# Identity products in five TensorE waits of a two-layer transformer step, and a later start for part of its constants

## What is computed

```python
sh1, sc1, g1, sh2, sc2, g2 = split(silu(cond) @ w_ada[l] + b_ada[l], 6)   # one cond for context, one for latents
h = rms_norm(x, norm1_g) * (1 + sc1) + sh1
q_lat, ckv_raw, krope, conv_in, na_qkv = split(h @ w_in)
q = rms_norm(rms_norm(q_lat, q_a_g) @ w_q_up); k, v = from(rms_norm(ckv_raw) @ w_kv_up, krope)
o = concat(attention(q, k, v), conv_module(conv_in), neighbourhood_attention(na_qkv))
x = x + g1 * (o @ w_out)
h = rms_norm(x, norm2_g) * (1 + sc2) + sh2
x = x + g2 * moe(h)        # sigmoid router, 16 experts in 4 groups, two of one group per token
```

## Time and profile before

| | |
|---|---|
| median of 3 runs | 1256.28 us |
| the profiled execution's own time | 1256.0 us |
| its span in the profile | 1254.2 us |
| TensorE (PE) busy | 1127.8 us, 90% of the span |
| VectorE (DVE) busy | 885.6 us, 71% |
| ScalarE (ACT) busy | 657.8 us, 52% |
| GpSimd (POOL) busy | 260.3 us, 21% |
| chain that ended last | PE 66%, DVE 21%, DMA 6%, issue 4% |
| mean granted TensorE clock | 0.931 of full speed |

### The profile page before, as it was taken

The page is one execution under the profiler, slowest core; times in us unless marked ns, Lnnn a source line. Parts: engine busy times, 40 slices in busy tenths (PEclk is TensorE's granted clock), DMA queues, the critical chain, the costliest instruction groups (busy, mean ns, idle before and its releaser), DMA issues.

```text
span 1254.2 us, 15896 instructions
## 1 busy us (share of the span) xinstructions
PE 1127.8 (90%) x6102; PEld 918.6 (73%) x6102; DVE 885.6 (71%) x1115; ACT 657.8 (52%) x910; POOL 260.3 (21%) x218
## 2 busy tenths in 40 slices
PE   5999998989689999999969898788949999999985
PEld 2787767678568888888857775577847888888863
DVE  1138177642579999998963767871378999998894
ACT  2222154431268788888833124442237778888870
POOL 5001110210114122212153021101021322212133
PEclk9999998979889999999989997787969999999997
DMA  9965774732489999999943321014358999999951
GB/s 359 305 230 206 300 318 182 276 153 100 168 298 373 353 385 383 370 388 386 396 175 86 120 77 63 4 41 168 117 208 332 357 377 380 375 379 376 372 245 51
DMA packets 54174, 320.72 MB, mean 256 GB/s; under 512 B 11498, under 2 KB 11610, under 8 KB 18896
## 3 DMA queue, kind: packets, MB, share of 16 engines
q1 hardware_dynamic: 38448, 276.59, 57.6%
q0 software_dynamic: 15648, 43.08, 9.4%
HBM read 313.40 MB, written 25.44 MB: 270 GB/s over the span
## 4 chain that ended last, share of the span: by engine, by line
PE 66%; DVE 21%; DMA 6%; issue 4%; ACT 1%; POOL 1%; SPq 0%; DVEq 0%; POOLq 0%; ACTq 0%
PE bank L1121 33%; PE bank L821 10%; PE bank L1034 6%; DVE w_lo L2109 5%; PE bank L810 4%; DMA ring<-wring_dram 3%; DVE conv_acc L1905 3%; PE bank L927 2%; PE bank L1113 2%; PE bank L899 2%; DMA late<-y_rows 2%; PE bank L832 1%; PE bank L913 1%; DVE rowmax L1705 1%; PE bank L865 1%
## 5 line engine op out<-in xcount | busy, mean ns | idle before, releaser
L2109 DVE TENSOR_TENSOR w_lo<-ring,w_hi 128x2048 fp32r<-128x2048 f32 x190 | 433.5, 2300 | 44.2 <-ACT w_hi L1420 44.0
L1420 ACT CAST w_hi<-ring 128x2048 fp32r<-128x2048 f32 x192 | 367.0, 1917 | 34.1 <-PE bank L1121 33.7
L1121 PE MATMUL bank<-w_hi,hgT_hi 128*128 128x512 f32 x512 | 204.5, 399 | 5.3 <-issue 3.4
L1121 PE MATMUL bank<-w_hi,hgT_lo 128*128 128x512 f32 x512 | 201.3, 393 | 0.0
L1121 PE MATMUL bank<-w_lo,hgT_hi 128*128 128x512 f32 x512 | 200.8, 392 | 0.0
L821 PE MATMUL bank<-ring,hT 128*128 128x256 f32 (+1 forms) x672 | 140.7, 370 | 0.4 <-issue 0.4
L821 PEld LDWEIGHTS bank<-ring,hT 128*128 128x128 f32 x672 | 122.6, 191 | 16.5 <-issue 1.9
L1121 PE MATMUL bank<-w_hi,hidT_hi 128*128 128x512 f32 x256 | 103.9, 406 | 18.9 <-DVE y_split L2163 18.9
L720 POOL DMA_INDIRECT y_rows<-y,y_at x26 | 47.1, 1810 | 353.2 <-ACT y L1451 353.2
L1121 PEld LDWEIGHTS bank<-w_hi,hgT_hi 128*128 128x128 f32 x512 | 97.0, 190 | 26.5 <-issue 7.2
L1121 PEld LDWEIGHTS bank<-w_hi,hgT_lo 128*128 128x128 f32 x512 | 96.9, 189 | 21.0
(11 more groups left out here) (266 smaller groups left out, 1596.3 us busy)
## 6 DMA issues: line engine op xcount, KB each, us to landing
ring<-wring_dram SPq DMA_DIRECT2D x260, 1024.0 KB, 8.4
y_rows<-hg POOLq DMA_DIRECT2D x6, 1024.0 KB, 7.2
kT<-mod_dram POOLq DMA_DIRECT2D x4, 1024.0 KB, 8.5
late<-y_rows POOLq DMA_DIRECT2D x4, 1024.0 KB, 14.4
ring<-wring_dram SPq DMA_DIRECT2D x6, 640.0 KB, 7.6
h_rows<-h_tok POOLq DMA_DIRECT2D x6, 512.0 KB, 3.0
bias<-na_bias_dram POOLq DMA_DIRECT2D x32, 64.0 KB, 4.9
A<-mod_dram POOLq DMA_DIRECT2D x2, 1024.0 KB, 5.0
```

Source lines behind the costliest of these rows:

```text
L1121: mm = pe.matmul(b[:, :], a, w[m], start=(start and k == 0), stop=(stop and k == 2))
L1420: act.copy(w_hi[:, q, :], in_ring(l, expert_slot(e, i))).then_inc(hi_made[q], 1)
L2109: dve.tensor_tensor(w_lo[:, q, :], in_ring(l, expert_slot(e, i)), w_hi[:, q, :], ALU.subtract) \
```

## The change

A new helper on TensorE, `keep_busy(l, key, count)`, waits until the bank that `key` names is free and then multiplies the identity by the identity `count` times into its first 128 columns. It raises no semaphore, nobody reads the result, and the next real product into that bank starts a new accumulation. It stands in five places of each layer, ahead of the waits listed above: 3 products (layer 0) or 14 (layer 1) behind the latents' transposes, 9 behind the mix transposes, 26 behind the last score product, 7 before each of the first two lists, 8 before the first expert's tokens.

At the start, layer 0's order on TensorE is rewritten: `turn_mod` of a pair comes between the two slots of the next pair, and the transposes of tiles 0 and 1 come before the eighth slot's products. `psum_plan` follows. Of the constants only the shapes and `vecs` are issued at first; triangle, row ids, router weights and bias, rotary tables, mask and the two tables are issued by GpSimd after `mod_ready`, ahead of the small transfers and the bias, which thereby also come after `mod_ready`. VectorE waits for the later constants behind the modulation of tile 2 and makes there what depends on them.

```diff
+IDLE_ROUTER, IDLE_LISTS, IDLE_GATHER, IDLE_MIX, IDLE_LATENTS = 26, 7, 8, 9, (3, 14)
...
+        for i, (m, k) in enumerate(FIRST_PAIRS):
+            order += [("ada", m, 2 * k)]
+            if i:
+                order += [("mod", *FIRST_PAIRS[i - 1])]
+            if i == len(FIRST_PAIRS) - 1:
+                order += first_turns
+            order += [("ada", m, 2 * k + 1)]
+        order += [("mod", *FIRST_PAIRS[-1])]
...
-        N_CONST = 16 * 8
+        N_CONST, N_CONST_LATER = 16 * 2, 16 * 6
...
-            pool.dma_start(triangle, shape_consts[:, 2, :]).then_inc(consts_loaded, 16)
-            pool.dma_start(wr[:], w_router).then_inc(consts_loaded, 16)
-            pool.dma_start(br[:], b_router.partition_broadcast(P)).then_inc(consts_loaded, 16)
-            pool.dma_start(ropes[:], rope).then_inc(consts_loaded, 16)
-            pool.dma_start(mask[:], na_mask).then_inc(consts_loaded, 16)
-            pool.dma_start(ids[:], row_ids).then_inc(consts_loaded, 16)
...
-            for n in range(DEPTH):
-                pool.dma_start(tables[n], no_token).then_inc(tables_cleared, 16)
...
+                else:
+
+                    pool.wait_ge(sems["mod_ready"], nth(l, "mod_ready", 1))
+                    pool.dma_start(triangle, shape_consts[:, 2, :]).then_inc(later_consts_loaded, 16)
+                    pool.dma_start(ids[:], row_ids).then_inc(later_consts_loaded, 16)
+                    pool.dma_start(wr[:], w_router).then_inc(later_consts_loaded, 16)
+                    pool.dma_start(br[:], b_router.partition_broadcast(P)).then_inc(later_consts_loaded, 16)
+                    pool.dma_start(ropes[:], rope).then_inc(later_consts_loaded, 16)
+                    pool.dma_start(mask[:], na_mask).then_inc(later_consts_loaded, 16)
+                    for m in range(DEPTH):
+                        pool.dma_start(tables[m], no_token).then_inc(tables_cleared, 16)
                 pool.dma_start(rowv[:], rows[n].partition_broadcast(P)) \
...
+            def keep_busy(l, key, count):
+
+                pe.wait_ge(*once_free(l, key))
+                for _ in range(count):
+                    pe.matmul(bank[bank_no(l, key)][:, 0:P], iden[:], iden[:], start=True, stop=True)
...
-                turn_normed(0)
-                turn_normed(1)
+                if n == 0:
+                    for i, (m, k) in enumerate(FIRST_PAIRS):
+                        ada_sums(l, m, 2 * k)
+                        if i:
+                            turn_mod(l, *FIRST_PAIRS[i - 1])
+                        if i == len(FIRST_PAIRS) - 1:
+                            pe.wait_ge(consts_loaded, N_CONST)
+                            pe.wait_ge(consts_made, N_MADE)
+                            turn_normed(0)
+                            turn_normed(1)
+                        ada_sums(l, m, 2 * k + 1)
+                    turn_mod(l, *FIRST_PAIRS[-1])
+                else:
+                    turn_normed(0)
+                    turn_normed(1)
                 first_projection(0)
...
+                keep_busy(l, ("q", 0, 0), IDLE_LATENTS[n])
                 pe.wait_ge(*once_read(l, ("ql", 1)))
...
+                keep_busy(l, ("out", 0, 0), IDLE_MIX)
                 pe.wait_ge(*once_read(l, ("mix", 5)))
...
+                keep_busy(l, ("place",), IDLE_ROUTER)
                 pe.wait_ge(sems["chosen"], nth(l, "chosen", 1))
-                pe.wait_ge(*once_free(l, ("place",)))
...
+                keep_busy(l, ("list", 0), IDLE_LISTS)
                 list_rows(0)
+                keep_busy(l, ("list", 1), IDLE_LISTS)
                 list_rows(1)
+                keep_busy(l, ("X0", 0), IDLE_GATHER)
...
+                    dve.wait_ge(later_consts_loaded, N_CONST_LATER)
+                    dve.tensor_copy(earlier[:], triangle)
+                    dve.tensor_copy(unit[:], ones[:])
```

More of the change, by code:

```diff
@@ L161, in pairs @@
             open_pair[:] = [(m, k)]
+    first_turns = [("n1", t, q) for t in range(2) for q in range(2)]
     if n == 0:
[L164 to L167, removed]
+        for i, (m, k) in enumerate(FIRST_PAIRS):
[7 more added lines that the diff above has]
+    else:
+        order += first_turns
     for j in range(5):
@@ L915, in turn_mod, with ada_sums @@
                 mm.then_inc(bank_full[bank_no(l, ("mod", m, k))], 1)
+            def ada_sums(l, m, s):
+                pe.wait_ge(*once_loaded(Layer(m), s))
+                w = in_ring(Layer(m), s).rearrange("p (k n) -> p k n", k=KC)
+                pe.wait_ge(*once_free(l, ("ada", m, s)))
+                b = bank[bank_no(l, ("ada", m, s))]
+                for c in range(KC):
+                    g = 32 * (c % 4)
+                    mm = pe.matmul(b[g:g + 32, 0:256], cond_p[:, c, :], w[:, c, :], start=(c < 4), stop=(c >= 4))
+                mm.then_inc(bank_full[bank_no(l, ("ada", m, s))], 1)
             def modulation(l, pairs):
@@ L920, in modulation @@
                     for s in (2 * k, 2 * k + 1):
[L921 to L928, removed]
+                        ada_sums(l, m, s)
                     for p in open_pair:
@@ L942, in _ @@
                 l = Layer(n)
[L944 to L948, removed]
                 def turn_normed(t):
@@ L1845, in _ @@
                 .then_inc(cond_ready, 1)
-            dve.tensor_copy(earlier[:], triangle)
-            dve.tensor_copy(unit[:], ones[:])
-            dve.tensor_copy(row_less[:], ids[:, 0:TILES]).then_inc(rows_known, 1)
-            dve.wait_ge(rows_known, 1)
-            dve.tensor_scalar(tile_row[:], row_less[:], row_less[:, 0:1], float(P - NO_TOKEN), ALU.subtract, ALU.add) \
-                .then_inc(rows_known, 1)
-            dve.tensor_scalar(row_v[:, :, :, 0], row_less[:, 0:1].unsqueeze(1).broadcast_to([P, TILES, NE]), -float(P), None, ALU.add)
-            dve.wait_ge(rows_known, 2)
-            dve.tensor_copy(row_v[:, :, :, 2], last(tile_row[:], NE))
             def ada_bias(l, n, lo, k):
@@ L1884, in _ @@
                         modulate(l, t)
+                    dve.wait_ge(later_consts_loaded, N_CONST_LATER)
+                    dve.tensor_copy(earlier[:], triangle)
+                    dve.tensor_copy(unit[:], ones[:])
+                    dve.tensor_copy(row_less[:], ids[:, 0:TILES]).then_inc(rows_known, 1)
+                    dve.wait_ge(rows_known, 1)
+                    dve.tensor_scalar(tile_row[:], row_less[:], row_less[:, 0:1], float(P - NO_TOKEN), ALU.subtract, ALU.add) \
+                        .then_inc(rows_known, 1)
+                    dve.tensor_scalar(row_v[:, :, :, 0], row_less[:, 0:1].unsqueeze(1).broadcast_to([P, TILES, NE]), -float(P), None, ALU.add)
+                    dve.wait_ge(rows_known, 2)
+                    dve.tensor_copy(row_v[:, :, :, 2], last(tile_row[:], NE))
                 def square_latents(q):
```

1 line of the change is left out of this document (added).

## The result

The changed kernel takes 1244.7 us (median of 4 runs, 1240.65 to 1248.56) against 1256.8 (4 runs, 1255.76 to 1259.68): a ratio of 0.9900, 95% interval 0.9864 to 0.9935. That is 12.1 us faster, where 13.5 was forecast, and 2.1 above the 1242.6 that was named.

The account below looks back on a forecast made before the run. It took the opening to be bound by memory (the eighth `w_ada` slot), then TensorE nearly everywhere except attention heads, partly slowed by low clock. Start 4.5 + bridges 9.0 = 13.5 us off 1256.0; named median 1242.6, range 1236.5 to 1250.5.

Parts of the forecast that it names:

- The slot: Start: the eighth `w_ada` slot lands earlier as small transfers leave the queue; 3.2 us, low bound 2.1, high 5.
- The steps behind it: Start, between the eighth slot's products and the first projection: fewer steps on the path; gain 3.3 us, bounds 1.8 and 5.3.
- the start as a whole: Opening of layer 0: 3.2 + 3.3 - 2.0 = 4.5 us gained, bounds 0.4 and 10.
- The cold projection: Start: waits behind the eighth slot leave the first projection at a low clock; loss 2 us, bounds 0 and 3.5.
- The bridges: Identity products in five waits per layer keep TensorE's clock up; 11.3 us if all hold, 9.0 taken.
- the first expert of layer 1: Layer 1's first expert at full clock: 2.5 us, and 1.1 for the transposes before it.
- the allowance of 2.3: Taken off the bridges for layer 0's router bridge starting at low clock, gaps between lists, and layer 1's mix starting low.
- Attention: Attention heads: low-clock stretches fall on other instructions; 3 us either way, no sign.
- Cover: Start: constants issued later by GpSimd delay nothing, as VectorE's next work was 20.96 us away; cost nothing.
- The second: Rival: the bridges don't hold the clock and only the start's 4.5 remain; 1251.5 us, chance 0.12.
- The third: Rival: the start gives only 0.4 us, with 9.0 from the bridges; 1246.6 us, chance 0.14.
- The fourth: Rival: identity products start cold, run late and push real work away; 1271 us, chance 0.06.

Follow-up runs that it names:

- e1: The kernel before with the identity products in all five places and its start as it was; 1247.1 us (ratio 0.9936).
- e2_start_only: The kernel after with all identity product counts at 0, so only the new start order and late constants; 1253.7 us (ratio 0.9976).
- e5_transposes: The kernel after with each identity product replaced by two transposes of the identity; 1242.1 us (ratio 0.9877).
- e11_old_order_bridges: The kernel after with the opening's order as before; late constants and all five bridges stay; 1243.2 us (ratio 0.9903).
- e3: The kernel before with the constants issued late, old order of the start, no identity products; 1252.5 us (ratio 0.9974).
- e6: The kernel after plus 2 identity products ahead of the start's last turn_mod and 10 ahead of the first projection; 1241.4 us (ratio 0.9876).
- e4: The kernel before with only TensorE's new start order, constants early, no identity products; 1254.6 us (ratio 0.9982).
- e8: The kernel after without the identity products at router, lists and gather; those of mix and latents stay; 1245.0 us (ratio 0.9902).
- e7: The kernel after with 60 identity products instead of 26 in each layer's router bridge; 1255.1 us (ratio 0.9993).
- e12_all: e9_last_expert plus three bridges in layer 0's attention heads (18, 11 and 10 identity products); 1229.6 us (ratio 0.9781).
- e9_last_expert: e6 plus 39 identity products ahead of the last expert's down products in both layers and 10 in layer 1's opening; 1233.4 us (ratio 0.9827).

## Why the prediction was right, point by point

- *The number.* 1242.6 does not follow from the sum: the median before, 1256.28, less 13.5 is 1242.8.
- *The slot.* Forecast 3.2 us earlier, and right: in the traces with late constants it lands between 29.1 and 29.7, with early ones at 32.3 (e1) to 33.5. But the prediction had TensorE wait for it, and that wait does not exist. With the new order TensorE comes from the seventh slot through products, `turn_mod` and 16 transposes, and gets to the eighth slot's products as it lands when it is warm, and 3 us after when it is cold (`e2_start_only`, 0.50 from 26 to 32, and `e5_transposes`, 0.51 from 25.6 to 32.6). The prediction saw the danger of a cold clock behind the slot only.
- *The steps behind it.* Forecast 3.3; from 9.94 us between the slot's products and the projection to 4.91, so 5.0. The modulation that the transposes used to hide is 1.52 us, near the half of 2.90 taken. The 1.7 over the forecast lies in shorter records: the slot's products took 1.07 for 1.94 and `turn_mod` 1.04 for 1.84. That this is clock is an estimate from the durations. `e11_old_order_bridges` has 1.94 and 1.84 at a granted clock of 0.50 (29.3 to 35.8), but in the trace of before the clock reads 1.00 here (33.5 to 40), as in the kernel after. So the start as a whole is worth 6.0 us in the trace and 3.3 in its cold form, and the forecast of 4.5 lies between the two by luck; the median of `e2_start_only` says 3.1.
- *The cold projection.* Forecast 2.0, measured 3.0 (6.73 - 3.69). This term was mis-sized in the direction that its upper bound of 3.5 had named; e3 and e11 (4.03 and 3.71) show that it comes of the new order, e6 that 12 identity products remove it.
- *The bridges.* The forecast was 9.0; the stages give 1.7 + 2.4 + 2.2 + 1.4 + 1.4 = 9.1, and alone they measured 9.8. The step that failed is one term: the first expert of layer 1 was to bring 3.6 and brought 1.4, as the clock fell during its first products. At 12.73 us it is above the 12 that the prediction had named as a sign of being wrong. The reason given for the allowance of 2.3, a late start of the router bridge in layer 0, did not occur: there 52 records took 6.05 us at a clock of 1.00. The loss came in the other layer, between gather and first expert, where the trace has 1.28 and 1.01 us of waits around 8 short transposes, and only in some executions: e1 and e5 have the same waits (1.33 and 1.39, then 1.01) and 11.17 us. That the allowance and this loss are nearly the same size is luck.
- *Attention.* ±3 without sign: 3.1 us shorter and 3.6 longer, which cancel, also by luck. `e6_start_bridge`, with the same code in the heads, has 0.1 us in layer 1 in place of 3.6. The 3.1 of layer 0 sit in one place. Behind a wait of 1.4 us for a `w_ada` slot (151.5 before, 145.6 after) 28 transposes take 4.93 us before, with the clock at 0.50 from 153 to 155, and 3.10 after, at 1.00 from 147 to 150. Over all traces that row has 3.10 in six (after, e1, e3, e4, e8, e11) and 4.6 to 5.1 in the other eight, with and without bridges, so this is where the clock happens to fall, no effect of the change.
- *Not in the sum.* The end of layer 0 takes 1.9 us more, from two causes. The last expert's down products take 7.59 us in place of 6.43, cold for longer behind their wait (10.4 us, before 9.5): the clock reads 0.50 from 632.5 to 635 and 0.71 to 640, before 0.50 from 643.8 to 646 and 0.91 to 650.3. And two transfers of rows follow one another in the chain, 8.04 + 19.45 = 27.5 us before and 28.9 after, and the experts' lead waits for them, of which 0.9 us reaches those down products. The 0.8 of layer 1's opening are its first projection, 5.38 us in the chain in place of 4.31, less a faster transpose step. The transfers:

```profile
587.55 9.16 DMA y_rows<-y,y_at
...
598.03 19.70 DMA late<-y_rows
```

- *Cover.* The later constants cost nothing: VectorE's next work after them, beside the earlier trace rows, still waits 20.16 us for the projection in its timeline:

```profile
63.94 0.96 DVE L1952 TENSOR_TENSOR probs<-proj 128x768 f32<-128x768 f32 x1 [20.16 <-ACT proj L1419]
```

- *Rivals.* The second (bridges don't hold the clock) fell with e1, e5 and the windows at 1.00, save in the first expert of layer 1, where it came true in part. The third (start gives nothing) was near in one of its parts, the cold projection, and by the medians the start is worth 3.1, between its 0.4 and the forecast's 4.5. The fourth (products late) did not happen, but e7 showed its price to be real: 10.4 us for 34 more products in each layer. The argument against it, that only long rows of full-width products had brought the clock back, does not fit, where it read 0.98 behind transposes alone.

What stays open: whether the late constants alone or the order alone is the better opening. By the medians they are 4.3 and 2.3 us, both ± 2; in one trace each, tile 1's transposes are 5.6 and 1.5 us ahead of before. Open too is what decides whether the clock falls in the first expert of layer 1, since the same waits had either outcome.

## What to carry to other kernels

Look for equal work with unequal durations in the chain of waits, and at the idle time ahead of the slow one. If nothing else can be put there, products on data at hand kept TensorE's clock here and were worth the cold stretch that they removed (14.05 us in place of 15.74 and 16.43 for the output product), save in the first expert of layer 1, where five of nine traces had it cold. Part of it may be handed back further on, as with `e8_no_router`, so time the place alone. Count the products to end some tenths of a microsecond before the wait does (0.30 to 1.28 were left here), since nearly all of what is too many is paid (10.4 of 12.1 us with `e7_router_60`). Rank the places by what stands in the chain behind them: here the 9.5 us wait ahead of the last expert's down products, which the change left alone, was worth more (about 6 us in two layers) than the 96 products at router, lists and gather. When steps are taken off the path, check what they had kept warm, and what the engine now has to do before the thing that it used to wait for. And price a cold stretch from several traces, since one kernel shows it warm in one execution and cold in the next.

## What the runs showed of the hardware

- In the router bridge 52 float32 transposes held the granted clock at 1.00 for 5.87 us (`e5_transposes`, 328.06 to 333.93), as 52 records of ordinary products did for 6.05 us (the kernel after, 322 to 328).
- At a granted clock of 1.00 a 128-column record of the identity product started every 0.114 us (120 in 13.64 us, `e7_router_60`, 326.6 to 340.2).
- Executions of one kernel spread over 3 to 14 us here (1240.65 to 1248.56 after, four runs; 1245.62 to 1259.85 for `e2_start_only`, twelve). In the traces the clock falls at different instructions of the same code, and a stretch of code is short in some and long in others: from the seventh slot's landing to the eighth slot's products 3.9 to 7.1 us, the first expert of layer 1 behind its bridges 11.2 or 12.7, the 28 transposes near 148 us 3.1 or 4.6 to 5.1. The narrowest spread is that of the kernel with most waits bridged: 1227.83 to 1230.87 for `e12_all`, six runs; but `e9_last_expert`, with nearly as many, has 8.3 us in five runs.
- The small transfers cost more than their bytes here: with them moved behind it, the eighth slot took 14.5 to 15.0 us from issue to landing (eleven kernels), with them beside it 17.4 to 18.7 (before, e1, e4). They are 0.9 MB, which is 2.1 us at the 0.42 MB per us that the ring alone moved in the kernel after.
- Some waits may have no room for a bridge: at the first heads of layer 1 TensorE waits 4.1 us while, by the plan, all eight banks hold something unread. This was read off the plan and not run.
